# Rows of x loaded first, state-space discretisation merged and moved behind the first norm, first two weight tiles interleaved

## The chip, the cores and the metric

The kernel runs on one core of one Trainium2 chip. The metric is device time in microseconds (us), the median of several runs of the whole program. A core has TensorE (PE, the matmuls), VectorE (DVE), ScalarE (ACT), GpSimd (POOL) and SyncE (SP), each with a program of its own; SP only issues DMAs here.

## The reference

Two transformer-like blocks over 1024 tokens of width 1024, float32 throughout. The part that the change touches is the start of the first block: 16 meta tokens are put ahead (1040 rows), an RMS norm, the input projection, and a state-space branch on its first 512 columns:

```python
h = rmsnorm(x, g_pre)                 # x * rsqrt(mean(x*x) + eps) * g
proj = h @ w_in
u, q, k, v, o, gi, gf, ga, gb = jnp.split(proj, IN_SPLITS, axis=-1)
dt = exp(log_dt); mag = exp(lam_re * dt)          # s5_ssm: "discretisation"
ab_re, ab_im = mag * cos(lam_im * dt), mag * sin(lam_im * dt)
z = ((ab - 1) * conj(lam)) / |lam|^2;  bb = z * b # complex
x_t = ab * x_(t-1) + bb u_t                       # complex scan over the tokens
y_a = gelu(Re(c x_t) + d * u_t);  y_a *= sigmoid(y_a @ w_glu)
```

Behind it come an mLSTM, branch and output projections, a gated feed-forward part with a convolution, and a second block (RWKV, dilated attention, feed-forward). Nothing of those is touched.

## The kernel before

**Tiling.** Activations lie transposed, 128 features on the partitions and 1040 columns of tokens, in `HB[:, k, :]` for k = 0..7. The columns are cut in three chunks c0, c1, c2 of 264, 264 and 512 (`CH1`). A dense product goes by tiles of 128 output features: a 512 KB weight tile `w_raw` comes by DMA from SP, ScalarE rounds it to `w_hi` (`split_act`), VectorE takes the rest `w_lo = w_raw - w_hi` (`split_dve`), and TensorE makes three matmuls for each k (hi·hi, hi·lo, lo·hi), 24 for a chunk and 72 for a tile. There are two `w_raw` and three `w_hi`/`w_lo` buffers. The input projection (`IN1`) has 24 tiles, t0 to t23: four u, four v, four o, eight q/k (t12 to t19), four g; then one tile "gates", then the tiles of the glu.

**The norm.** `prenorm_act` squares each row block of x in three chunks into one of the six-chunk temporaries (`ssm_VX`, `m_S`, `m_S`, `m_G`), `prenorm_pe` sums over the partitions with a matrix of ones, ScalarE takes the root in two steps (Ln, Exp), VectorE makes y = x·g·root into a temporary, ScalarE copies it rounded into `XHA`/`XHB`, and VectorE writes the rest into `XLA`/`XLB`. c0 and c1 lie in XHA/XLA, c2 in XHB/XLB.

**The first tiles.** t0, t1, t2 are run as nine groups in the order of `FIRST`: c0 of all three, c1 of all three, c2 of all three, so that TensorE can start while the norm of c1 and c2 is still made.

**The state-space branch** rides in the background. It is a generator for each engine (`ssm_pe`, `ssm_act`, `ssm_dve`); every chunk of the main work calls `tick()`, which runs RS = 3 steps, up to the next three `yield`s. What lies between two yields is issued as a piece, and each engine executes its instructions in the order issued. `pause(n)` skips n steps, and PRE, MID and POST set how long. On VectorE the generator makes the discretisation ("one" with 16 columns, "two" with 256), `bb`, `Bn`, the table E of powers over 130 blocks (into HB), then for each group j = 0..3 of u: `powers(j)`, `outputs(j)` (the array `ssm_W`), `ssm_Dop`, and the X chain with the scan. ScalarE turns them into the matmul operands `ssm_Bop` (`inputs`) and `ssm_Cop` (`outputs`), copies the results "bu" and applies the gelu. TensorE has three pieces for each j: "k" (16 matmuls of `ssm_Cop` and `ssm_Bn`), "bu" (64) and "ys" (eight steps of 2 to 16 matmuls on `ssm_Dop` and `ssm_Cop`).

**Order and waits at the start.** POOL issues the eight row blocks of x; SP issues `ssm_p1`, `ssm_p2` (640 KB), waits for x3, and then issues the first two weight tiles and `ssm_bc1`; ScalarE issues `cst` (612 KB, with the matrix of ones and the identity) and `vecs`. `step()` calls inside the norm put the discretisation between its squares; on VectorE all of it stands ahead of the two first `w_lo`. The DVE program of `first_dve` ticks nine times, 27 steps, before it takes `w_lo` of t3 and later tiles. A q or k tile goes through one buffer `m_G`: ScalarE evicts the three chunks into it, VectorE convolves (one TENSOR_SCALAR, three SCALAR_TENSOR_TENSOR over 1040 columns), and the next tile's eviction waits for that. PSUM has a ring of four banks for the dense chunks and one of four for the background.

## Time and profile before

| | us |
|---|---|
| median of 3 runs | 3365.61 (3361.63 to 3368.23) |
| the profiled execution | 3363.58 |
| its span | 3361.8 |
| TensorE busy in it | 3217.5 (96%) |
| VectorE busy | 1713.1 (51%) |
| ScalarE busy | 1219.6 (36%) |
| POOL busy | 74.6 (2%) |
| mean granted TensorE clock | 0.99 |

Times inside the trace are counted from the span's start. A timeline row is: start, duration, engine, line, operation, what it writes and reads, the form (partitions x elements), how many in a row, and in brackets how long the engine stood idle before and who released it. The listing with its line numbers is the one printed above. A float32 or fp32r matmul shows as one or more records in the trace.

### The profile page before, as it was taken

The numbers are of one execution on the slowest core, as the hardware profiler recorded it, in microseconds if no ns is written. First come the engines' busy times: TensorE is split into PE (matmuls) and PEld (weight loads), VectorE is DVE, ScalarE is ACT, GpSimd is POOL, SyncE is SP. The second block draws the span as 40 slices with busy tenths as digits, with TensorE's granted clock in tenths as the row PEclk, the third lists the DMA queues.
The fourth block names the chain that finished last, engine by engine and source line by source line (L and its number), as shares of the span: only waits on it lengthen the run. The fifth ranks groups of instructions, "written<-read, shape, count | busy, mean of one in ns | idle before, by whom it ended". The sixth has DMA issues, their size and how long they took to land.

```text
span 3361.8 us, 56145 instructions
## 1 busy us (share of the span) xinstructions
PE 3217.5 (96%) x24028; PEld 2678.6 (80%) x24028; DVE 1713.1 (51%) x3196; ACT 1219.6 (36%) x2166; POOL 74.6 (2%) x148
## 2 busy tenths in 40 slices
...
GB/s 106 60 68 64 67 86 66 77 58 139 160 107 90 55 49 46 51 44 82 136 177 157 125 86 93 29 23 24 18 14 119 94 91 54 46 50 45 55 94 113
DMA packets 85624, 262.36 MB, mean 78 GB/s; under 512 B 10592, under 2 KB 10720, under 8 KB 85248
## 3 DMA queue, kind: packets, MB, share of 16 engines
...
q14 instruction: 58, 0.48, 0.0%
...
## 4 chain that ended last, share of the span: by engine, by line
PE 79%; DVE 11%; ACT 7%; issue 2%; DMA 1%; DVEq 0%; SPq 0%; POOL 0%; ACTq 0%; POOLq 0%
PE ps L127 76%; PE ps L126 2%; DVE HB L166 2%; DVE w_lo L166 1%; PE ps L135 1%; ACT w_hi L163 1%; ACT L145 1%; DVE HB L176 1%; ACT m_D L145 1%; DVE C L176 1%; ACT a_PT L163 0%; DVE m_SS L176 0%; DVE XLA L166 0%; DMA m_D<-mq 0%; ACT L150 0%
## 5 line engine op out<-in xcount | busy, mean ns | idle before, releaser
L166 DVE TENSOR_TENSOR w_lo<-w_raw,w_hi 128x1024 fp32r<-128x1024 f32 (+3 forms) x353 | 393.5, 1115 | 384.2 <-ACT w_hi L163 382.1
L127 PE MATMUL ps<-XHA,w_hi 128*128 128x264 f32 (+3 forms) x1456 | 467.8, 321 | 37.4 <-DVE w_lo L166 33.2
L163 ACT ACTIVATE w_hi<-w_raw 128x1024 fp32r<-128x1024 f32 (+3 forms) x353 | 339.9, 963 | 340.9 <-PE ps L127 281.2
L127 PE MATMUL ps<-XLA,w_hi 128*128 128x264 f32 (+3 forms) x1456 | 457.7, 314 | 0.0
L127 PE MATMUL ps<-XHA,w_lo 128*128 128x264 f32 (+3 forms) x1456 | 456.2, 313 | 0.0
L127 PE MATMUL ps<-XHB,w_hi 128*128 128x512 f32 x920 | 369.9, 402 | 6.4 <-DVE w_lo L166 3.7
L127 PE MATMUL ps<-XHB,w_lo 128*128 128x512 f32 x920 | 360.2, 391 | 0.0
L127 PE MATMUL ps<-XLB,w_hi 128*128 128x512 f32 x920 | 360.1, 391 | 0.0
L127 PEld LDWEIGHTS ps<-XHA,w_hi 128*128 128x128 f32 x1456 | 276.3, 190 | 68.4 <-issue 43.3
L127 PEld LDWEIGHTS ps<-XLA,w_hi 128*128 128x128 f32 x1456 | 276.2, 190 | 21.1 <-issue 3.6
L127 PEld LDWEIGHTS ps<-XHA,w_lo 128*128 128x128 f32 x1456 | 276.6, 190 | 16.5
L127 PEld LDWEIGHTS ps<-XHB,w_hi 128*128 128x128 f32 x920 | 173.6, 189 | 49.7 <-issue 9.4
L127 PEld LDWEIGHTS ps<-XHB,w_lo 128*128 128x128 f32 x920 | 173.5, 189 | 37.2
L127 PEld LDWEIGHTS ps<-XLB,w_hi 128*128 128x128 f32 x920 | 173.7, 189 | 36.0 <-issue 1.9
L166 DVE TENSOR_TENSOR HB<-HB,ps 128x512 f32<-128x512 f32 (+1 forms) x136 | 88.5, 655 | 213.0 <-PE ps L127 213.0
L127 PE MATMUL ps<-X2HA,w_hi 128*128 128x512 f32 x416 | 163.6, 393 | 2.1 <-DVE w_lo L166 2.1
L127 PE MATMUL ps<-X2HB,w_hi 128*128 128x512 f32 x416 | 162.7, 391 | 0.0
L127 PE MATMUL ps<-X2LA,w_hi 128*128 128x512 f32 x416 | 162.5, 391 | 0.0
L127 PE MATMUL ps<-X2HA,w_lo 128*128 128x512 f32 x416 | 162.4, 390 | 0.0
L127 PE MATMUL ps<-X2HB,w_lo 128*128 128x512 f32 x416 | 161.9, 389 | 0.0
L127 PE MATMUL ps<-X2LB,w_hi 128*128 128x512 f32 x416 | 161.8, 389 | 0.0
L173 DVE TENSOR_SCALAR C<-G,vecs 128x512 f32<-128x512 f32 x88 | 48.0, 546 | 212.8 <-ACT G L163 212.8
...
## 6 DMA issues: line engine op xcount, KB each, us to landing
...
```

The costliest lines, as they stand in the source:

```text
L126: return Issued(e.matmul(out, a, b, start=start, stop=stop, skip_group_check=True))
L127: return Issued(e.matmul(out, a, b, start=start, stop=stop))
L135: return Issued(self.eng and self.eng.transpose(out, src, ident))
L145: return Issued(self.eng and self.eng.activation(out, src, func, **kw))
L163: return Issued(self.eng and self.eng.activation(out, src, ACT.Copy))
L166: return Issued(self.eng and self.eng.tensor_tensor(out, a, b, op))
L173: return Issued(self.eng.tensor_scalar(out, a, s1, s2, op0, op1))
L176: return Issued(self.eng and self.eng.scalar_tensor_tensor(out=out, in0=a, scalar=s, in1=b, op0=op0, op1=op1))
```

## The change

**Loads.** SP issues x0, x2, x4, the first weight tile, x6, the second, the merged parameters `ssm_p2` (680 KB), the third tile, and `ssm_bc1`. ScalarE issues x1, x3, x5, x7 and `vecs`. `cst` is loaded by POOL once x6 and x7 have landed. The ones are written by a VectorE memset.

**Norm.** Each row block is squared whole (x7 in three chunks) into buffers of its own, `squares`, which overlay the later X area. VectorE adds the squares of x2 and x3, and of x4 and x5, so that the sums take 18 matmuls in place of 24. The first root comes ahead of the copies, the second and third stand between them, and so do the splits of t1 and t2. One table load stands at the start; the two parts of the discretisation brought four others.

**Discretisation.** "One" and "two" are one array of ND = 272 columns, treated once. It is no longer in the norm: the DVE generator starts behind it, and is cut in short steps (`cmul_steps` yields twice within a complex product).

**Ticks.** `first_dve` ticks only for c2: three ticks, nine steps, before `w_lo` of t3. PRE goes from 42 to 82, POST from 8 to 4, EASE = 2 is new, and the pauses around `inputs(0)` and `outputs(0)` are new.

**First tiles.** `first_order` runs t0 and t1 in c0 interleaved: four k of t0, then t0 and t1 by turns, then four k of t1. The eight matmuls ahead of them are 128 columns wide, on the ones, in place of 256 on the identity.

```diff
-LAG, K0, RS, RM, NG, PRE, MID, POST, HN, Q5 = 9, 1, 3, 5, 4, 42, 18, 8, 8, 1
+LAG, RS, RM, NG, PRE, MID, POST, HN, Q5 = 9, 3, 5, 4, 82, 18, 4, 8, 1
+EASE = 2
...
+def cmul_steps(V, S, outr, outi, ar, ai, br, bi, t1, t2):
+    V.tt(outr, ar, br, MUL).then_inc(S)
+    a = V.tt(t1, ai, bi, MUL).then_inc(S)
+    yield
+    V.tt(outi, ar, bi, MUL).then_inc(S)
+    b = V.tt(t2, ai, br, MUL).then_inc(S)
+    yield
+    V.wait_ge(S, a)
+    V.tt(outr, outr, t1, SUB).then_inc(S)
+    V.wait_ge(S, b)
+    V.tt(outi, outi, t2, ADD).then_inc(S)
...
+SUMS = [(0,), (1,), (2, 3), (4, 5), (6,), (7,)]
...
-    for k in range(8):
+    P.wait_ge(S.dve, "ones")
+    for n, ks in enumerate(SUMS):
+        k = ks[0]
         for c, (c0, cn) in enumerate(CH1):
-            n, b = K.tmp1.take(P, k, False)
-            P.wait_ge(S.act, ("sq", k, c))
-            P.mm(K.fg["pn", "sum", c][:, 0:cn], K.ones, b[:, 0:cn], k == 0, k == 7).then_inc(S.pe, ("sq", k, c))
-        P.step(K0)
+            P.wait_ge(S.act, ("sq", ks[-1], c))
+            if len(ks) > 1:
+                P.wait_ge(S.dve, ("pair", k))
+            op = P.mm(K.fg["pn", "sum", c][:, 0:cn], K.ones, K.squares[k][:, c0:c0 + cn], n == 0, n == len(SUMS) - 1)
+            if n == len(SUMS) - 1:
+                op.then_inc(S.pe, ("sum", c))
...
 def prenorm_act(A, K):
     S = K.pn
-    A.step(3)
+    A.table(LN_EXP)
     for k in range(8):
         A.wait_ge(K.x[k], "x")
-        for c, (c0, cn) in enumerate(CH1):
-            n, b = K.tmp1.take(A, k, True)
-            A.act(b[:, 0:cn], K.HB[:, k, c0:c0 + cn], ACT.Square).then_inc(S.act, ("sq", k, c))
-            K.tmp1.done(n, (S.pe, ("sq", k, c)))
-        A.step(K0 if k < 5 else 0)
-        if k in FIRST_W:
-            split_act(A, K, FIRST_W.index(k))
-    A.table(LN_EXP)
+        for n, (c0, cn) in enumerate(CH1 if k == 7 else [(0, T1)]):
+            A.act(K.squares[k][:, c0:c0 + cn], K.HB[:, k, c0:c0 + cn], ACT.Square).then_inc(S.act, ("sq", k, n))
+        if k < 7:
+            S.act.at["sq", k, 1] = S.act.at["sq", k, 2] = S.act.n
+        if k == 5:
+            split_act(A, K, 0)
+    A.wait_ge(K.c.pool, END)
...
+        A.wait_ge(S.pe, ("sum", c))
...
+    def between(c, k):
+        if c == 0 and k == 1:
+            split_act(A, K, 1)
+        if c == 0 and k in (4, 6):
+            root(k // 2 - 1)
+        if c == 0 and k == 7:
+            split_act(A, K, 2)
+            s = ssm_views(K)
+            A.wait_ge(K.ssm_ld, END)
+            A.act(s.dt, s.p[:, 2, :], ACT.Exp).then_inc(K.ssm.act, "dt")
+
     root(0)
-    root(1)
     for c, (c0, cn) in enumerate(CH1):
-        normalise_act(A, K, S, c, c0, cn, K.tmp1)
-        if c == 0:
-            root(2)
-            split_act(A, K, 2)
+        for k in range(8):
+            n, b = K.tmp1.take(A, k, False)
+            A.wait_ge(S.dve, ("y", c, k))
+            A.cp(S.X.hi(k, c0, cn), b[:, 0:cn]).then_inc(S.act, ("hi", c, k))
+            between(c, k)
...
-    V.step(8 * K0)
-    for i in range(2):
-        split_dve(V, K, i)
-    K.tmp1.n[V] = 24
-    for k in range(8):
-        V.wait_ge(K.x[k], "x")
+    for a, b in ((2, 3), (4, 5)):
+        V.wait_ge(S.act, ("sq", b, 0))
+        V.tt(K.squares[a], K.squares[a], K.squares[b], ADD).then_inc(S.dve, ("pair", a))
+    split_dve(V, K, 0)
...
+        if c == 0 and k == 3:
+            split_dve(V, K, 1)
...
+ND = 272
...
 def ssm_sp(D, K):
-    D.dma(K.ssm_p1[:, :, :], K.I["ssm_p1"]).then_inc(K.ssm_ld, by=16)
-    D.dma(ssm_views(K).p2, K.I["ssm_p2"]).then_inc(K.ssm_ld, by=16)
-    D.wait_ge(K.x[3], "x")
+    for k in (0, 2, 4):
+        D.dma(K.HB[:, k, 0:T1], K.I["x1"][:, k, :]).then_inc(K.x[k], "x", by=16)
     load_weight(D, K, 0)
+    D.dma(K.HB[:, 6, 0:T1], K.I["x1"][:, 6, :]).then_inc(K.x[6], "x", by=16)
     load_weight(D, K, 1)
+    D.dma(K.ssm_BT[:, 0:3 * ND + 512], K.I["ssm_p2"]).then_inc(K.ssm_ld, by=16)
+    load_weight(D, K, 2)
     D.dma(K.ssm_bc1[:, :, :, :], K.I["ssm_bc1"]).then_inc(K.ssm_bl, by=16)
...
+def discretise_act(A, K, S, s):
+    A.wait_ge(S.dve, "den")
+    A.act(s.mag, s.den, ACT.Exp).then_inc(S.act, "mag")
+    yield from pause(22)
+    for name, out in (("sn", s.sn), ("cs", s.cs)):
+        A.wait_ge(S.dve, name)
+        A.act(out, out, ACT.Sin).then_inc(S.act, name)
     yield
-    A.wait_ge(S.dve, (tag, "den"))
-    A.act(mag, den, ACT.Exp).then_inc(S.act, (tag, "mag"))
-    for name, out in (("sn", sn), ("cs", cs)):
-        A.wait_ge(S.dve, (tag, name))
-        A.act(out, out, ACT.Sin).then_inc(S.act, (tag, name))
-        yield
...
+def discretise_dve(V, K, S, s):
...
+    V.tt(zr, lr, lr, MUL).then_inc(d)
+    V.tt(kc, li, li, MUL).then_inc(d)
...
+    V.recip(den, den).then_inc(d)
+    yield
+    V.wait_ge(S.act, "cs")
...
-    yield
-    yield from pause(10)
-    while P.hold:
-        yield
-    yield from pause(8)
     yield from pause(PRE)
...
+    yield from discretise_act(A, K, S, s)
...
-    yield from pause(8)
-    yield from pause(33)
+    yield from pause(PRE - 23 - 11)
     inputs(0)
-    yield from pause(8)
+    yield from pause(9)
     outputs(0)
-    yield from pause(PRE - 41)
+    yield from pause(2)
...
+    yield from discretise_dve(V, K, S, s)
+    one = lambda a: a[:, 256:ND]
+    two = lambda a: a[:, 0:256]
+    mag1, c1, n1, ar1, ai1, zr1, zi1 = [one(a) for a in (s.mag, s.cs, s.sn, s.ar, s.ai, s.zr, s.zi)]
+    ar2, ai2, zr2, zi2 = [two(a) for a in (s.ar, s.ai, s.zr, s.zi)]
+    V.after(d)
+    yield from cmul_steps(V, d, K.ssm_bb2[:, 0, :], K.ssm_bb2[:, 1, :], zr2, zi2, s.b2[:, 0, :], s.b2[:, 1, :], q1[:, 0, :], q1[:, 1, :])
     yield
-    yield from discretise_dve(V, K, S, "one", K.ssm_p1[:, 0, :], K.ssm_p1[:, 1, :], s.one)
...
-    cmul(V, d, K.ssm_bb2[:, 0, :], K.ssm_bb2[:, 1, :], zr2, zi2, s.p2[:, 3, :], s.p2[:, 4, :], q1[:, 0, :], q1[:, 1, :])
...
+    V.wait_ge(K.c.cst, END)
+    yield from cmul_steps(V, d, sq(K.ssm_bb1[:, 0, :]), sq(K.ssm_bb1[:, 1, :]), b16(zr1), b16(zi1), bc1[:, 0], bc1[:, 1],
+                          sq(q1[:, 0, :]), sq(q1[:, 1, :]))
+    yield
...
-    yield
-    while V.hold:
-        yield
...
-    def outputs(j):
+    def outputs(j, often):
...
-            if tau % 2 == 1:
+            if often or tau % 2 == 1:
                 yield
     yield from powers(0)
-    yield from pause(23)
-    yield from outputs(0)
-    yield from pause(PRE - 38)
+    yield from outputs(0, True)
+    yield from pause(EASE)
...
+def first_order():
+
+    both = [(0, 0, k) for k in range(4)]
+    for k in range(4, 8):
+        both += [(0, 0, k), (0, 1, k - 4)]
+    both += [(0, 1, k) for k in range(4, 8)]
+    return both + [(c, t, k) for c, t in FIRST[2:] for k in range(8)]
...
-    for n, (c, t) in enumerate(FIRST):
+    begun = []
+    for c, t, k in first_order():
...
+        if (c, t) not in begun:
+            b = first_ring(K, len(begun)).take(P, ("u", t, c))
+            if not begun:
+                for _ in range(8):
+                    P.mm(b[:, 0:128], K.ones, K.ones, True, True)
+            begun.append((c, t))
+            P.wait_ge(K.w.act, ("hi", i))
+            P.wait_ge(K.w.dve, ("lo", i))
+        b = first_ring(K, FIRST.index((c, t)))["u", t, c]
+        ready(k, c)
+        x, y = K.X.hi(k, c0, cn), K.X.lo(k, c0, cn)
+        P.mm(b[:, 0:cn], wh[:, k, :], x, k == 0, False)
+        P.mm(b[:, 0:cn], wh[:, k, :], y, False, False)
+        op = P.mm(b[:, 0:cn], wl[:, k, :], x, False, k == 7)
+        if k == 7:
+            op.then_inc(S.pe, ("u", t, c))
+            K.used[i] = (S.pe, ("u", t, c))
+            P.tick()
+            P.u_done += c == 2
+    P.wait_ge(K.c.cst, END)
...
 def first_dve(V, K):
     next_tile(V, K, split_dve)
     for c, t in FIRST:
-        V.tick()
+        if c == 2:
+            V.tick()
...
-    for i in (2, 3, 4):
+    for i in (3, 4):
...
-    for k in range(8):
-        G.dma(K.HB[:, k, 0:T1], K.I["x1"][:, k, :]).then_inc(K.x[k], "x", by=16)
     G.mset(K.small[:, 0:1], 1e-6).then_inc(K.c.pool)
     G.mset(K.small[:, 1:2], 64e-5).then_inc(K.c.pool)
     G.mset(K.small[:, 2:3], 1.0).then_inc(K.c.pool)
     G.mset(K.small[:, 4:6], 0.0).then_inc(K.c.pool)
     G.mset(K.G1[:, 0:3], 0.0).then_inc(K.gpad)
+    G.wait_ge(K.x[6], "x")
+    G.wait_ge(K.x[7], "x")
+    G.dma(K.cst[:, 256:1224], K.I["cst"][:, 256:1224]).then_inc(K.c.cst, by=16)
+    G.dma(K.cst[:, 0:128], K.I["cst"][:, 0:128]).then_inc(K.c.cst, by=16)
     G.wait_ge(K.c.cst, END)
...
 def act_program(A, K):
-    A.dma(K.cst[:, :], K.I["cst"]).then_inc(K.c.cst, by=16)
+    for k in (1, 3, 5, 7):
+        A.dma(K.HB[:, k, 0:T1], K.I["x1"][:, k, :]).then_inc(K.x[k], "x", by=16)
     A.dma(K.vecs[:, :], K.I["vecs"]).then_inc(K.c.vec, by=16)
+    prenorm_act(A, K)
+    A.wait_ge(K.c.vec, END)
     A.bg.append(ssm_act(A, K))
-    A.step()
-    A.wait_ge(K.c.pool, END)
-    A.wait_ge(K.c.vec, END)
-    prenorm_act(A, K)
-    A.hold, A.rate = False, RS
+    A.rate = RS
...
 def dve_program(V, K):
+    V.mset(K.ones, 1.0).then_inc(K.pn.dve, "ones")
+    prenorm_dve(V, K)
     V.bg.append(ssm_dve(V, K))
-    V.step()
-    V.wait_ge(K.c.cst, END)
-    V.wait_ge(K.c.vec, END)
-    prenorm_dve(V, K)
-    V.hold, V.rate = False, RS
+    V.rate = RS
...
-    o["ssm_p1"] = np.stack([one(lr), one(li), one(ldt)], axis=1)
...
-    o["ssm_p2"] = np.stack([rep(lr), rep(li), rep(ldt), o2(bre), o2(bim)], axis=1)
+    o["ssm_p2"] = np.concatenate([f(a) for a in (lr, li, ldt) for f in (rep, one)] + [o2(bre), o2(bim)], axis=1)
```

**VectorE, the first `w_lo` behind the norm.** `ssm_W` is what `powers(0)` writes. Before, the end of `powers(0)` and four `w_lo` in a row:

```order
L166 TENSOR_TENSOR ssm_W<-ssm_W,ssm_q 128x64 [waits s_ssm_dve] x2
L166 TENSOR_TENSOR ssm_W<-ssm_W,ssm_a 128x64 [waits s_ssm_dve]
L166 TENSOR_TENSOR ssm_q<-ssm_W,ssm_a 128x64
L166 TENSOR_TENSOR ssm_W<-ssm_W,ssm_a 128x64
L166 TENSOR_TENSOR ssm_q<-ssm_W,ssm_a 128x64
L166 TENSOR_TENSOR ssm_W<-ssm_W,ssm_q 128x64 [waits s_ssm_dve] x2
L166 TENSOR_TENSOR w_lo<-w_raw,w_hi 128x1024 [waits s_w_act] x4
L186 COPY ssm_W<-ssm_bc 128x64 [waits s_ssm_dve,s_ssm_act]
```

In the changed kernel, the discretisation of 272 columns and the first `w_lo` behind the norm:

```order
L167 TENSOR_TENSOR ssm_Cop<-ssm_BT 128x272 x2
L167 TENSOR_TENSOR ssm_Cop<-ssm_Cop 128x272 [waits s_ssm_dve,s_ssm_act]
L184 RECIPROCAL ssm_Cop<-ssm_Cop 128x272 [waits s_ssm_dve]
L167 TENSOR_TENSOR w_lo<-w_raw,w_hi 128x1024 [waits s_w_act]
L167 TENSOR_TENSOR ssm_a<-ssm_Cop 128x272 [waits s_ssm_act]
L167 TENSOR_TENSOR ssm_a<-ssm_Cop 128x272
L173 TENSOR_SCALAR ssm_Cop<-ssm_a 128x272 [waits s_ssm_dve]
L167 TENSOR_TENSOR ssm_Cop<-ssm_Cop,ssm_BT 128x272 [waits s_ssm_dve]
```

`w_lo` of t3 stood behind the whole of E and `powers(0)`, 162 rows behind the norm's last; now it stands 18 rows behind it, and one `w_lo` comes every few rows.

**ScalarE, the squares.** `ssm_VX`, `m_S` and `m_G` are the temporaries of the squares, `ssm_Cop` is the discretisation's scratch. Before:

```order
L145 ACTIVATE ssm_VX<-HB 128x264 [waits s_x_in0]
L145 ACTIVATE ssm_VX<-HB 128x264
L145 ACTIVATE m_S<-HB 128x512
L145 ACTIVATE m_S<-HB 128x264 [waits s_x_in1]
L145 ACTIVATE m_G<-HB 128x264
L145 ACTIVATE m_G<-HB 128x512
L145 ACT_TABLE_LOAD
L145 ACTIVATE ssm_Cop<-ssm_BT 128x256
L145 ACTIVATE ssm_VX<-HB 128x264 [waits s_pn_pe,s_x_in2]
L145 ACTIVATE ssm_VX<-HB 128x264 [waits s_pn_pe]
L145 ACTIVATE m_S<-HB 128x512 [waits s_pn_pe]
L145 ACTIVATE ssm_Cop<-ssm_Cop 128x256 [waits s_ssm_dve]
```

Changed:

```order
L151 ACT_TABLE_LOAD
L146 ACTIVATE squares<-HB 128x1040 [waits s_x_in0]
L146 ACTIVATE squares<-HB 128x1040 [waits s_x_in1]
L146 ACTIVATE squares<-HB 128x1040 [waits s_x_in2]
L146 ACTIVATE squares<-HB 128x1040 [waits s_x_in3]
L146 ACTIVATE squares<-HB 128x1040 [waits s_x_in4]
L146 ACTIVATE squares<-HB 128x1040 [waits s_x_in5]
L164 ACTIVATE w_hi<-w_raw 128x1024 [waits s_w_raw0]
L146 ACTIVATE squares<-HB 128x1040 [waits s_x_in6]
L146 ACTIVATE squares<-HB 128x264 [waits s_x_in7]
L146 ACTIVATE squares<-HB 128x264
L146 ACTIVATE squares<-HB 128x512
```

The discretisation's activations and table loads are gone from between the squares, and a row block is one instruction.

**TensorE, the piece k of j = 0.** With row numbers, since the matmuls read alike. Before, behind the last chunk of t5 and ahead of the first of t6:

```order
453 L127 MATMUL ps<-XLB,w_hi 128x512
454 L127 MATMUL ps<-XHB,w_lo 128x512
455 L126 MATMUL ps<-ssm_Cop,ssm_Bn 32x256 [waits s_ssm_dve,s_ssm_act]
456 L126 MATMUL ps<-ssm_Cop,ssm_Bn 32x256 x7
457 L127 MATMUL ps<-XHA,w_hi 128x264 [waits s_w_dve,s_w_act,s_in1_act]
458 L127 MATMUL ps<-XLA,w_hi 128x264
```

Changed, inside t9, behind its c0:

```order
689 L128 MATMUL ps<-XLA,w_hi 128x264
690 L128 MATMUL ps<-XHA,w_lo 128x264
691 L127 MATMUL ps<-ssm_Cop,ssm_Bn 32x256 [waits s_ssm_dve,s_ssm_act]
692 L127 MATMUL ps<-ssm_Cop,ssm_Bn 32x256 x7
693 L128 MATMUL ps<-XHA,w_hi 128x264 [waits s_in1_act]
694 L128 MATMUL ps<-XLA,w_hi 128x264
```

The piece moved from between two tiles to behind the first chunk of a tile, more than three tiles later.

## Rows read from the trace of the kernel before

**Rows 1.** TensorE waits, 34 to 650 us: us in total, times, longest us.
```profile
PE ps L127 <- DVE w_lo L166: 27.7, 1, 27.7
...
PE ps L126 <- ACT ssm_Cop L145: 3.7, 1, 3.7
PE ps L127 <- DVE ssm_Dop L186: 2.8, 2, 1.5
```

**Rows 2.** Windows: busy us of each engine, TensorE clock, DMA share, GB/s.
```profile
18.00:20.00 2.00, 2.00 (x8) 1.32 (x7) 1.79 (x7) 1.62 (x3) 0.00 (x0) 1.00 1.03 412
20.00:22.00 2.00, 2.00 (x9) 1.21 (x8) 1.83 (x6) 1.56 (x4) 0.00 (x0) 1.00 0.13 49
...
80.00:90.00 10.00, 0.00 (x0) 0.00 (x0) 9.80 (x36) 0.00 (x0) 0.00 (x0) 0.50 0.00 0
99.00:103.00 4.00, 3.81 (x17) 3.84 (x18) 1.18 (x2) 0.56 (x1) 0.00 (x0) 0.50 0.69 203
...
138.00:144.00 6.00, 4.84 (x29) 3.57 (x30) 3.17 (x6) 2.06 (x2) 0.00 (x0) 0.50 0.40 144
212.00:276.00 64.00, 64.00 (x625) 56.13 (x624) 41.22 (x128) 19.23 (x30) 0.00 (x0) 1.00 0.19 67
```

**Rows 3.** Timeline of TensorE at the start: start us, us, line, operation.
```profile
15.21 2.79 PE L127 MATMUL ps<-m_S,cst 128*128 128x512 f32 x4
...
20.29 1.47 PE L127 MATMUL ps<-m_S,cst 128*128 128x512 f32 x4
...
34.22 0.36 PE L127 MATMUL ps<-XHA,w_hi 128*128 128x264 f32 x1
```

**Rows 4.** Timeline of ScalarE at the start.
```profile
9.86 1.28 ACT L145 ACT_TABLE_LOAD   x1
11.18 0.21 ACT L145 ACTIVATE ssm_s<-ssm_s 128x16 f32<-128x16 f32 x1
...
28.79 0.93 ACT L145 ACTIVATE m_G<-HB 128x264 f32<-128x264 f32 x2
...
31.04 0.48 ACT L145 ACTIVATE m_S<-ps,small 128x264 f32<-128x264 f32 x1
```

**Rows 5.** DMA issues up to 40 us: KB each, us to landing.
```profile
HB<-in_x POOLq DMA_DIRECT2D x8, 520.0 KB, 9.4
```

**Rows 6.** Timeline of VectorE at the start.
```profile
16.91 0.43 DVE L166 TENSOR_TENSOR ssm_Cop<-ssm_BT,ssm_Cop 128x256 f32<-128x256 f32 x1 [1.69 <-ACT ssm_Cop L145]
...
22.50 0.29 DVE L173 TENSOR_SCALAR ssm_Cop<-ssm_Cop 128x256 f32<-128x256 f32 x1
...
25.27 1.75 DVE L183 RECIPROCAL ssm_Cop<-ssm_Cop 128x256 f32<-128x256 f32 x1
...
32.66 0.89 DVE L176 SCALAR_TENSOR_TENSOR ssm_VX<-HB,vecs,m_S 128x264 f32<-128x264 f32 x2
```

**Rows 7.** Timeline of VectorE, 57 to 100 us.
```profile
57.48 1.47 DVE L166 TENSOR_TENSOR XLB<-m_G,XHB 128x512 fp32r<-128x512 f32 x2
...
97.83 2.35 DVE L166 TENSOR_TENSOR w_lo<-w_raw,w_hi 128x1024 fp32r<-128x1024 f32 x2
```

**Rows 8.** Timeline of ScalarE around 136 us.
```profile
135.48 0.60 ACT L145 ACTIVATE m_S<-ps 128x512 f32<-128x512 f32 x1 [5.09 <-PE ps L127]
136.71 1.25 ACT L145 ACTIVATE ssm_Cop<-ssm_W,cst 128x1152 f32<-128x1152 f32 x1 [0.63 <-DVE ssm_W L166]
```

**Rows 9.** Timeline of VectorE, 299 to 350 us.
```profile
306.39 1.31 DVE L166 TENSOR_TENSOR ssm_BT<-ssm_BT,HB 128x520 f32<-128x520 f32 x2 [1.04 <-ACT ssm_BT L163]
...
317.27 0.07 DVE L192 MEMSET ssm_VX<- 128x8 f32 x1
...
332.17 0.20 DVE L186 COPY ssm_W<-ssm_bc 128x64 f32<-128x64 f32 x1 [2.25 <-ACT ssm_Bop L145]
...
341.73 3.98 DVE L176 SCALAR_TENSOR_TENSOR m_S<-m_G,vecs,m_S 128x1040 f32<-128x1040 f32 x3
```

**Rows 10.** Timeline of ScalarE, 322 to 358 us.
```profile
354.36 2.40 ACT L145 ACTIVATE ssm_Cop<-ssm_W,cst 128x1152 f32<-128x1152 f32 x2
```

More of the change, by code:

```diff
@@ L512, in prenorm_dve @@
     for c, (c0, cn) in enumerate(CH1):
         V.wait_ge(S.act, ("sd", c))
-        normalise_dve(V, K, S, K.HB, K.rs0, c, c0, cn, "g_mix_pre", K.tmp1)
+        for k in range(8):
+            n, b = held[k] = tmp.take(V, k, True)
+            V.stt(b[:, 0:cn], K.HB[:, k, c0:c0 + cn], K.vec("g_mix_pre", k), K.rs0[:, c0:c0 + cn], MUL, MUL).then_inc(
+                S.dve, ("y", c, k))
+            if k:
+                rest(c, k - 1, c0, cn)
+        rest(c, 7, c0, cn)
         if c == 0:
@@ L668, in ssm_act @@
     S, s = K.ssm, ssm_views(K)
-    yield
-    yield from discretise_act(A, K, S, "one", K.ssm_p1[:, 2, :], s.one)
-    yield from discretise_act(A, K, S, "two", s.p2[:, 2, :], s.two)
-    yield from pause(2)
-    while A.hold:
-        yield
+    yield from discretise_act(A, K, S, s)
     def inputs(j):
@@ L778, in ssm_dve @@
             V.after(d)
-            cmul(V, d, E[:, 0, at, n:n + k], E[:, 1, at, n:n + k], E[:, 0, at, 0:k], E[:, 1, at, 0:k], bc(cur[0]), bc(cur[1]),
-                 qa, qb)
+            many = cmul_steps if w * k > 200 else cmul_whole
+            yield from many(V, d, E[:, 0, at, n:n + k], E[:, 1, at, n:n + k], E[:, 0, at, 0:k], E[:, 1, at, 0:k],
+                            bc(cur[0]), bc(cur[1]), qa, qb)
         n += k
@@ L883, in ssm_dve @@
             yield from pause(3)
-            yield from outputs(j + 1)
+            yield from outputs(j + 1, False)
             yield from pause(MID - 18)
```

91 lines of the change are left out of this document (39 added, 52 removed), and 2 rows, old and new, of the table WARM.

## The prediction

> **What bounds the kernel now.** I read the busy shares first: TensorE is busy for 96% of the span and every other engine for about half or less, so TensorE sets the end, and the change can only gain what TensorE waits for or runs slowly through. All that is changed lies ahead of the glu, which TensorE begins at about 444 us; from there on the order of all engines is the same. So I read TensorE's waits from its first real matmul on [rows 1]: one of 27.7 us for a `w_lo`, one of 3.7 for `ssm_Cop`, two of 2.8 together for `ssm_Dop`. Then the start: the first real matmul is at 34.22 [rows 3], which is time without product work. Then the clock: TensorE is granted 0.50 in the windows at 80, 99 and 138 us [rows 2], thus 1.2 in place of 2.4 GHz, each time around a wait of rows 1. The sum is made against the profiled execution, 3363.6 us, which is 2.0 below the median of the three runs shown and inside their spread.
>
> **A: the start.** The rows of x come at 412 GB/s with the DMA share at 1.03, and by 20 to 22 us the share is down to 0.13 [rows 2]. But the last square begins at 28.79 [rows 4]: before, ScalarE is what is late, since the discretisation's activations and table loads stand between the squares and wait for VectorE. Now nothing stands there, so the end of the loads decides. Ahead of x6 on the queues are eight rows of x at 520 KB [rows 5], one weight tile and `vecs`, 4.9 MB; at 0.41 MB per us, from 2.7 us on (an estimate: at that pace the 7.2 MB of rows, parameters, constants and first two tiles are over at 20 us, as they are), and with 0.7 us to land, x6 is there at 15.3. Behind it: its square over 1040 columns, 1.1 (0.93 for the 776 columns of [rows 4], scaled); its sums, 1.9 (1.47 for 776 columns at full clock [rows 3]); the first chunk of x7's sums, 0.4; the root, 0.9, and hand-overs, 0.1; from the first y at 32.66 [rows 6] to the first matmul at 34.22 [rows 3], 1.6. That gives 21.3 in place of 34.22: **-12.9**. Bounds: 19.5, if x6 lands ahead of its share; 25, if the sums run at half clock to their end, as the first ones did (2.79 in place of 1.47 [rows 3]), and the row loads come no better than with everything else between them (20.2 us for all).
>
> On the two queues: the traffic ran at 412 GB/s with all row loads on one of them. The Trainium skill, "DMA: Bandwidth & Descriptors", section "Issuing engines are not separate DMA queues", says that issuing from several engines saves only the time of the issue; by that rule the split between SP and ScalarE gives nothing, and I book nothing for it. What term A books is the order: 2.2 MB of parameters, constants and later tiles leave the front.
>
> **B: the nine groups of t0 to t2.** They end at 71.5 (the wait of 27.7 begins there, as the `w_lo` pair at 97.83 takes 2.35 [rows 7]), 37.3 behind the first matmul. VectorE gets one more `w_lo` (2.35/2) into the norm of c0, and ScalarE gets two roots and a split between its copies. Interleaving t0 and t1 puts TensorE's work where the norm of c0 sets the pace, and gives some back. I take **+1.3**; bounds 0 and +2.4.
>
> **C: the wait of 27.7.** VectorE's norm ends at 58.9 [rows 7], and then 39 us of `bb`, E and powers stand ahead of `w_lo` of t3. Now it is 18 rows. Their price: the 256-column steps of "two" went from 16.91 to 22.79, 5.9 for 16 instructions [rows 6]; scaled by 272/256 6.1; three products and a sum more, 1.1; the RECIPROCAL 1.75 [rows 6]: 9.0. With the first matmul as zero the norm ends at 24.7 + 1.2 (the added `w_lo`) + 1.2 (waits for ScalarE) = 27.1, `w_lo` starts at 36.1 and ends at 37.3, and the nine groups end at 38.6. So it is there 1.3 ahead of need, and the next ones have a tile's time each (11.3) for under ten rows of work. The whole wait goes: **-27.7**; bound: 3 of it stay, if ScalarE's Exp or its `w_hi` comes late. **D:** behind the wait TensorE ran at 0.50 from 99.2 to 103 [rows 2]; without the idle time there is no drop: half of 3.8 us, **-2.0**.
>
> The 39 us of VectorE are not gone. They now run beside t3 to t8, and `outputs(0)` behind them. Six tiles are 68 us of TensorE, and before, VectorE was busy for 1.18 of the 4 us behind 99 [rows 2] and had `outputs(0)` and one split a tile up to 137. That is the cover.
>
> **E: k and Dop of j = 0.** Cop(0) is issued behind the c2 eviction of a tile (135.48) and was 0.63 late by VectorE at 136.71, then takes 2.4 [rows 8]; k stood at the tile's end and waited 3.7. Now k has one chunk of 264 columns, 2.9 us, between: 0.8 stays, **-2.9**. The window of 138 to 144 at 0.50 has 4.84 us of TensorE work [rows 2]: half of it, **-2.4**. The two waits for Dop, at the first ys, go, as ys is now over two tiles behind k: **-2.8** [rows 1].
>
> **F: what is late next.** PRE moves k, bu, ys by some three to four tiles, so that j = 1 and 2 fall into the q/k tiles t13 to t20, where VectorE also convolves and where the next tile's eviction waits for it. VectorE in such a stretch is busy for 41.2 of 64 us [rows 2]; enough in sum, but its order is fixed. I followed the order of the three engines with: X chain 11.0 (306.39 to 317.37), outputs 8.7 (332.17 to 340.9), convolution 4.9 (0.9 and the 3.98 of 341.73), Cop 2.4 [rows 9, 10], a table load of 1.3 from its start to the next activation's [rows 4]. With t9's start as zero, X(1) is done at 98, t14's convolution at 107.5, outputs(2) at 121.4, t15's convolution at 126.3, t16's at 134.2; then eviction, table load, gelu, and Cop(2) is done at 139.0. TensorE comes to k(2) at 135.4: it waits **+3.6**, and I take the clock drop of E again behind it, **+2.4**. k(1) and two bank waits behind convolutions: **+1.7**. Bounds for all of F: 0 and 14.
>
> The table load is 1.28, and the next activation begins 1.32 behind its start [rows 4]. The Trainium skill, "ScalarE: Activation LUTs", section "What ACT_TABLE_LOAD costs", adds a drain and gives 2.66 for each switch. By that page k(2) would wait 1.4 longer, and the sum would be 3323.3; here the trace disagrees with it.
>
> **Sum.** -12.9 + 1.3 - 27.7 - 2.0 - 2.9 - 2.4 - 2.8 + 3.6 + 2.4 + 1.7 = -41.7, and 3363.6 - 41.7 = **3322**.
>
> **Rivals.**
> 1. *F does not arise.* A few us of slack in VectorE's chain (a convolution that starts when its tile's eviction is done) let Cop(2) come in time. For: my count has hand-overs that overlap in the trace. Then 3322 - 7.7 = 3314.
> 2. *The start gains less.* The loads of weights and parameters share the bandwidth with the rows, and the sums run at half clock, since TensorE has less to do there (18 matmuls, not 24). For: the first sums at half clock [rows 3]. First matmul at 27 to 29 in place of 21.3: 3328 to 3330.
> 3. *The wait is not gone but moved.* `w_lo` of t3, or one of the next, still comes late by 5 to 15 us, as a short step behind it waits for ScalarE's Exp or Sin, which wait in ScalarE's own order behind an eviction. For: VectorE waits for ScalarE more than once ahead of t4's `w_lo`. Against: each takes 0.4 and a table load 1.3. 3330 to 3340.
> 4. *Slower than before.* The moved work is serialised with TensorE in the q/k stage. A q/k tile's convolution stands behind the X chain (11.0) and outputs (8.7 and the wait for Bop), the next tile's eviction behind the convolution, and TensorE has four banks, 13 us of chunks, ahead. If VectorE falls behind by over 13 us of slack, TensorE pays both blocks, about 20 us, in each of three j: 60, and the time is 3322 + 60 = 3382. Against: VectorE's four convolutions, X chain, powers, outputs and splits of one j are 52.5 us of 61.5. It decides once waits add 9 us to each j.
> 5. *Nothing moves* (the 27.7 are given back in a lump at the drain behind t23, where ys(3) now stands): the ys work is the same in either place, so this would need the last gelu to be late. 3355 to 3370.
>
> **How the numbers follow.** Forecast 0.50; rival 1 0.18; rival 2 0.16; rival 3 0.10; rival 4 0.03; rival 5 0.03. From 3308 (rival 1 and x6 early) to 3338 (rival 3 but for its end) holds all but about 0.12; the size of F and A is worked out from single rows, so I do not make it narrower. A difference under 0.2%, 6.7 us, is about what a measurement of this kernel cannot tell from none. Faster by more: all but rivals 4 and 5, and part of the latter, 0.95; within: 0.02; slower: 0.03.
>
> **What the profile of the changed kernel would show.** The first real matmul at 21 us, the last row's square ending by about 17 (A). No wait of TensorE for a `w_lo` above 1 us and clock 1.00 from the third tile on (C, D). `w_lo` of t3 at about 57 (B, C). The wait for `ssm_Cop` in two or three places with 0.5 to 4 us, the largest at the third k, and a window at 0.50 behind it (E, F). From the glu on, every tile at the same distance as before. The forecast is wrong if a wait for m_G or m_S evictions of several us turns up on TensorE between t12 and t20, or if the first matmul is behind 25 us.

## The result

| | before | changed |
|---|---|---|
| median, us (4 runs each) | 3363.62 (3360.52 to 3368.23) | 3321.56 (3317.30 to 3322.42) |
| ratio | | 0.9875 (95%: 0.986 to 0.989) |
| the profiled execution | 3363.58 | 3317.30 |
| its span | 3361.8 | 3315.2 |
| first real matmul | 34.22 | 21.38 |
| t0 to t2 done, t3 begins | 71.5, and 99.19 behind the wait | 59.38 |
| first matmul of the glu | 443.86 | 403.2 |

By the medians 42 us are gone, where 41.7 were forecast. By the first matmul of the glu, behind which no order of work changed, it is 40.7. The page's first part of the changed kernel, busy us, share of the span and instructions:

```profile
PE 3205.0 (97%) x24016; PEld 2668.3 (80%) x24016; DVE 1711.8 (52%) x3168; ACT 1207.9 (36%) x2140; POOL 71.5 (2%) x142
```

TensorE's share goes from 96 to 97%. Its waits from its first sums to 650 us (us in total, times, longest), which answer to [rows 1]:

```profile
PE ps L127 <- ACT ssm_Cop L146: 5.2, 3, 4.1
...
PE ps L128 <- DVE glu_l L167: 1.9, 2, 1.5
...
PE ps L128 <- ACT m_G L146: 1.5, 2, 0.8
PE ps L127 <- DVE ssm_VX L193: 1.4, 1, 1.4
PE ps L128 <- ACT XHA L164: 1.3, 1, 1.3
```

(`...` stands for lines left out.) No wait for a `w_lo` is left in this stretch, and none for `ssm_Dop`. `ssm_Cop` is now waited for three times, 4.1 us at the most. Windows (busy us of each engine, TensorE clock, DMA share, GB/s), which answer to [rows 2]:

```profile
14.00:16.00 2.00, 2.00 (x8) 1.14 (x6) 1.23 (x1) 1.31 (x3) 0.77 (x2) 1.00 1.04 414
25.00:28.00 3.00, 2.45 (x11) 2.48 (x12) 2.05 (x7) 2.55 (x6) 0.00 (x0) 0.52 0.49 175
60.00:100.00 40.00, 40.00 (x265) 36.93 (x264) 35.13 (x145) 10.59 (x16) 0.00 (x0) 1.00 0.25 93
100.00:130.00 30.00, 30.00 (x189) 27.20 (x188) 20.85 (x115) 9.96 (x14) 0.00 (x0) 1.00 0.21 77
270.00:275.00 5.00, 5.00 (x27) 3.65 (x27) 2.03 (x5) 0.05 (x1) 0.00 (x0) 0.66 0.00 0
```

TensorE is busy from 60 to 130 us without a gap at full clock. There VectorE is busy for 35.13 of 40 us: the 39 us of table and powers that TensorE waited for. Two windows are at half clock for a part: in c0 at 25 us and behind the third k at 270 us.

The start, on TensorE, ScalarE and VectorE (start, us, engine, line, operation), which answers to [rows 3], [rows 4] and [rows 6, 7]:

```profile
6.58 13.26 PE L128 MATMUL ps<-squares,cst 128*128 128x264 f32 x36 [6.58 <-ACT squares L146]
19.68 1.95 PE L128 MATMUL ps<-cst 128*128 128x128 f32 x16
21.38 0.37 PE L128 MATMUL ps<-XHA,w_hi 128*128 128x264 f32 x1
```

```profile
14.95 2.22 ACT L146 ACTIVATE squares<-HB 128x1040 f32<-128x1040 f32 x4 [0.69 <-DMA HB<-in_x]
18.64 0.48 ACT L146 ACTIVATE m_S<-ps,small 128x264 f32<-128x264 f32 x1 [1.47 <-PE ps L128]
```

```profile
46.78 0.44 DVE L167 TENSOR_TENSOR ssm_Cop<-ssm_BT,ssm_Cop 128x272 f32<-128x272 f32 x1
...
54.12 1.85 DVE L184 RECIPROCAL ssm_Cop<-ssm_Cop 128x272 f32<-128x272 f32 x1
55.89 1.16 DVE L167 TENSOR_TENSOR w_lo<-w_raw,w_hi 128x1024 fp32r<-128x1024 f32 x1
```

The last squares, of x6 and x7, begin at 14.95, and the root waits 1.47 us, for TensorE's sums, which run from 6.58 to 19.84 without a gap. The part of the discretisation that stands ahead of `w_lo` of t3 takes 46.78 to 55.89, 9.1 us (its last products come behind it), and `w_lo` of t3 is written 2.3 us before t3 can begin.

### The profile page after: what moved, and what is told of

Read it like the earlier page. It is cut to its first block, busy times and chain, and to the rows that moved or that the text cites. A ratio compares the mean times of both kernels' runs of the same rounds, so it can differ in the third digit from the quotient of the medians.

```text
span 3315.2 us, 56059 instructions
## 1 busy us (share of the span) xinstructions
PE 3205.0 (97%) x24016; PEld 2668.3 (80%) x24016; DVE 1711.8 (52%) x3168; ACT 1207.9 (36%) x2140; POOL 71.5 (2%) x142
## 4 chain that ended last, share of the span: by engine, by line
PE 79%; DVE 11%; ACT 7%; issue 2%; DMA 1%; DVEq 0%; SPq 0%; POOL 0%; ACTq 0%; POOLq 0%
PE ps L128 76%; PE ps L127 2%; DVE w_lo L167 1%; DVE HB L167 1%; PE ps L136 1%; ACT w_hi L164 1%; ACT L146 1%; DVE HB L177 1%; ACT m_D L146 1%; DVE m_S L177 1%; DVE C L177 1%; ACT a_PT L164 0%; DVE m_SS L177 0%; DMA m_D<-mq 0%; DVE ssm_q L167 0%
```

## The experiments

The times of before beside which each run was made had medians of 3359.6 to 3361.9. Since executions of one kernel spread over 2 to 11 us, I compare, beside the medians, three marks of each trace, where an edit at the start shows undisturbed: the first real matmul, the start of t3, and the first matmul of the glu (changed kernel: 21.38, 59.38, 403.2). There is one trace of each run, and the marks scatter too: four of the runs below (short steps undone, and the three on the places of k) leave the start as it is in the changed kernel, and together with it they have the first real matmul at 21.38 to 21.88 and t3 at 59.38 to 60.07. A difference of up to 0.7 us in these marks shows nothing.

### The ticks alone

```diff
 def first_dve(V, K):                    # the kernel before
     for c, t in FIRST:
-        V.tick()
+        if c == 2:
+            V.tick()
 def ssm_pe(P, K):
-    yield from pause(PRE)
+    yield from pause(PRE + 18)
 def ssm_act(A, K):
-    yield from pause(33)
+    yield from pause(33 + 18)
```

> The kernel before with one part of the change: VectorE's background ticks in the first nine groups only for c2 (9 steps ahead of w_lo of t3, not 27), and the TensorE and ScalarE pieces of the state-space work put 18 steps later to match. Loads, norm, discretisation, interleaving as before. My theory (terms C and D): the wait of 27.7 us for w_lo and its clock drop go, since 9 steps of bb, Bn and the first powers are about 10 us and VectorE is free at 58.9 against a need at 71.5; the 3.7 us wait for Cop(0) stays, as all is shifted alike; but the steps of E are long ones (9 steps of 1.7 to 2.8 us in a tile of 11.3), so up to 5 us come back at t4 to t6. About 3363.6 - 29.7 + 2 = 3336 (3333 to 3340). Rival (the merge and the short steps are what matters): waits of 10 us or more in t4 to t8, 3345 or above.

Measured: 3334.62 us (3333.47 to 3335.98), ratio 0.9917 (0.9902 to 0.9932). TensorE's waits up to 460 us:

```profile
PE ps L126 <- ACT ssm_Cop L145: 3.7, 1, 3.7
PE ps L126 <- DVE ssm_VX L192: 1.9, 1, 1.9
...
PE ps L127 <- DVE ssm_Dop L186: 1.5, 1, 1.5
```

No wait for `w_lo` at all, not even with long steps: `w_lo` of t3 starts at 68.20 and takes 1.22, and t3 begins at 71.32. The first real matmul stays at 34.22, and the glu begins at 415.5, 381.3 behind it; before it was 409.6, in the changed kernel 381.8. So 28 us of the gain (27.2 by the medians) come from one `if`, the number of steps ahead of `w_lo` of t3, with two pauses to match, and the merge, the short steps and the other places of k add nothing there. The tick edit without the two pauses was not tried; as I read the order, TensorE would then wait for Cop(0) with tiles held that VectorE's steps need to get on.

### Short steps undone

```diff
 def cmul_steps(V, S, outr, outi, ar, ai, br, bi, t1, t2):    # the changed kernel
-    V.tt(outr, ar, br, MUL).then_inc(S)
-    ...
+    cmul(V, S, outr, outi, ar, ai, br, bi, t1, t2)
+    yield
+    yield
```

> The changed kernel with whole complex products in one step again (the two yields of cmul_steps behind the product, so that the count of steps is the same). If nine steps and not their length are what brought w_lo of t3 in time, nothing moves: no wait of TensorE for w_lo, glu within 0.5 us of 403.2. Rival (the short steps are needed to get each w_lo out in time): waits for w_lo of 1 to 3 us at t4 to t8.

Measured: 3321.73 us (3316.10 to 3324.85), glu at 403.4, the same waits as the changed kernel's to 0.1 us. As expected, nothing moved. A whole product of 256 columns is some 2.1 us, and no wait for a `w_lo` came of it.

### The loads in the old order, and all on one queue

```diff
 def ssm_sp(D, K):                       # e3: the changed kernel
+    D.dma(K.ssm_BT[:, 0:3 * ND + 512], K.I["ssm_p2"]).then_inc(K.ssm_ld, by=16)
+    D.wait_ge(K.x[3], "x")
-    for k in (0, 2, 4):
-        D.dma(K.HB[:, k, 0:T1], K.I["x1"][:, k, :]).then_inc(K.x[k], "x", by=16)
...
 def act_program(A, K):
-    for k in (1, 3, 5, 7):
-        A.dma(K.HB[:, k, 0:T1], K.I["x1"][:, k, :]).then_inc(K.x[k], "x", by=16)
+    A.dma(K.cst[:, 256:1224], K.I["cst"][:, 256:1224]).then_inc(K.c.cst, by=16)
...
 def pool_program(G, K):
+    for k in range(8):
+        G.dma(K.HB[:, k, 0:T1], K.I["x1"][:, k, :]).then_inc(K.x[k], "x", by=16)
```

> The changed kernel with the loads in the old order: all rows of x on POOL, constants on ScalarE and the state-space parameters on SP at the very start. If the order of the bytes is what term A gained at the loads, the last row lands at about 19 to 20 us, the first real matmul is at 25 to 26 in place of 21.4, and the time is 4 to 5 us above the changed kernel's. Rival (ScalarE, not the loads, set the start in both kernels, so A came from taking the discretisation out of the squares): first matmul within 1 us of 21.4 and the same time.

```diff
 def ssm_sp(D, K):                       # e4: the changed kernel
-    for k in (0, 2, 4):
+    for k in range(6):
...
-    D.dma(K.HB[:, 6, 0:T1], K.I["x1"][:, 6, :]).then_inc(K.x[6], "x", by=16)
+    for k in (6, 7):
+        D.dma(K.HB[:, k, 0:T1], K.I["x1"][:, k, :]).then_inc(K.x[k], "x", by=16)
```

> The changed kernel with all eight rows issued by SP, in the same order of bytes (x0 to x5, first weight tile, x6, x7), none by ScalarE. If the queue does not matter, the DMA share stays near 1.0 at 410 to 430 GB/s, the first matmul is within 0.5 us of 21.4 and the time is the same. Rival (two queues share the bandwidth better or issue earlier): the first matmul 1 us or more later.

The first real matmul of the one and of the other:

```profile
25.79 0.37 PE L128 MATMUL ps<-XHA,w_hi 128*128 128x264 f32 x1
```

```profile
20.97 0.37 PE L128 MATMUL ps<-XHA,w_hi 128*128 128x264 f32 x1
```

Old order: 3326.06 us (3323.46 to 3328.85), first matmul 4.4 later, glu at 407.3, 4.1 later. One queue: 3322.19 us (3318.80 to 3322.84), first matmul 0.4 sooner. So of the 12.8 us of term A the order of the loads is 4.4; the other 8.4 stay with the old loads, and belong together to what no longer stands between the squares and to the fewer sums; no run takes these two apart. Both expectations held. The second queue is worth nothing. The Trainium skill, "DMA: Bandwidth & Descriptors", section "Issuing engines are not separate DMA queues", says that several issuing engines save no more than the time of the issue, and the trace agrees (20.97 with one, 21.38 with two).

### The sums of the squares

```diff
-SUMS = [(0,), (1,), (2, 3), (4, 5), (6,), (7,)]        # e12: the changed kernel
+SUMS = [(k,) for k in range(8)]
```

> The changed kernel without VectorE's additions of squares: 24 sum matmuls in place of 18. By term A the end of the start is set by what lands last (x6, x7), and 6 more sums of 0.6 us each ahead of them are done as the rows land: the first real matmul within 0.7 us of 21.4. Rival (TensorE is behind with its sums at half or full clock): 1 to 3 us later.

```diff
 def prenorm_pe(P, K):                   # e11: the changed kernel
-    for n, ks in enumerate(SUMS):
-        for c, (c0, cn) in enumerate(CH1):
+    last = len(SUMS) - 1
+    walk = ([(n, c) for n in range(last - 1) for c in range(3)]
+            + [(n, c) for c in range(3) for n in (last - 1, last)])
+    for n, c in walk:
```

> The changed kernel with the last sums by chunk: x6 and x7 for c0, then for c1, then for c2, in place of all of x6 and then all of x7. Term A has the whole of x6's sums (1.8 us) between its square and the first root. If TensorE's sums are what the first root waits for (1.47 us in the changed kernel), it comes up to 1.3 us sooner, as x7's first square is there by then: first real matmul at 20.2 to 20.8. Rival (x7's square is what is late): first matmul within 0.3 us of 21.4.

TensorE's start in the run without pairs, and in the run by chunk, and ScalarE's first root in each:

```profile
6.87 16.90 PE L128 MATMUL ps<-squares,cst 128*128 128x264 f32 x48 [6.87 <-ACT squares L146]
...
25.31 0.37 PE L128 MATMUL ps<-XHA,w_hi 128*128 128x264 f32 x1
```

```profile
22.57 0.48 ACT L146 ACTIVATE m_S<-ps,small 128x264 f32<-128x264 f32 x1 [5.12 <-PE ps L128]
```

```profile
20.12 1.95 PE L128 MATMUL ps<-cst 128*128 128x128 f32 x16
21.82 0.37 PE L128 MATMUL ps<-XHA,w_hi 128*128 128x264 f32 x1
```

```profile
17.77 0.48 ACT L146 ACTIVATE m_S<-ps,small 128x264 f32<-128x264 f32 x1 [0.17 <-PE ps L128]
```

Without pairs: 3326.93 us (3326.43 to 3330.73), the first root waits 5.12 us for the sums, and the first real matmul is 3.9 us later (0.3 of it in a later first square), the glu, at 407.2, 4.0. My expectation was wrong, and the rival's cause came about, beyond the 1 to 3 us that it gave: 24 sums keep TensorE busy for 16.9 us without a gap from its first square on, and end 6.3 us behind the last square. So two VectorE additions of 1.24 us are worth some 3.6 to 3.9 us, which I had booked at nothing. It is TensorE's own pace that counts here, and its first sums are slow in every trace. In the changed kernel:

```profile
7.00:11.00 4.00, 4.00 (x8) 2.41 (x8) 0.85 (x1) 2.78 (x4) 0.00 (x0) 1.00 1.02 419
13.00:17.00 4.00, 4.00 (x15) 2.53 (x14) 2.18 (x2) 3.10 (x5) 1.24 (x2) 1.00 1.04 419
```

Busy all the time in both windows, it gets 8 records done in the first and 15 in the second, while the granted clock reads 1.00 in both. The prediction calls such sums "at half clock"; the rows show half the pace, and not its cause.

By chunk: 3319.22 us (3315.42 to 3323.86), the root waits 0.17 in place of 1.47, and yet the first real matmul is at 21.82, where I had expected 20.2 to 20.8. The first `XLA` piece is ready at 20.25, but the matmul stands behind the warm-up matmuls, which stand behind all sums: TensorE's own queue is what is late. In the changed kernel these two are nearly level (the piece is ready at 21.10, the matmul starts at 21.38). VectorE's norm still began sooner, so that t3 begins at 58.35 and the glu at 402.6.

### The interleaving, and the clock in c0

```diff
 def first_order():                      # e5: the changed kernel
-    both = [(0, 0, k) for k in range(4)]
-    ...
+    both = [(0, t, k) for t in range(2) for k in range(8)]
```

> The changed kernel with t0 and t1 one after the other in c0 (the order of before), all else as changed. If interleaving gives TensorE work while the norm of c0 sets its pace, the nine groups end 1 to 2.9 us later than 59.4 and the time is as much longer, unless the clock drop at 25 us changes. Rival (the norm of c1 and c2 on VectorE sets the end of the nine groups anyway): nothing moves by more than 0.5 us.

Measured: 3323.04 us (3318.71 to 3325.20). The glu is at 405.8, 2.6 us later, and t3 begins 40.7 us behind the first matmul, in place of 37.8 to 38.2. But the trace shows half clock from 26.7 to 33.6 us, and from 28.6 on TensorE waits for nothing until t3, so that up to 2.5 us of the difference can be the clock. So the interleaving is worth 0.4 to 2.9 us by this trace, and whether the longer drop comes of the order itself no run shows; the medians can't tell either.

```diff
 def first_pe(P, K, ready):              # e8: the changed kernel
+        if (c, t, k) == (0, 0, 4):
+            early = first_ring(K, 1).take(P, ("u", 1, 0))
+            for _ in range(12):
+                P.mm(early[:, 0:128], K.ones, K.ones, True, True)
```

> The changed kernel with twelve matmuls of 128 columns on the ones (1.5 us, their result is overwritten) between the fourth and fifth k of t0, where TensorE idles for 1.29 us, the last of several gaps in c0, and falls to half clock from 25.1 to 28.5. If the gap brings the drop, the window at 25 to 28 shows 1.00 and the nine groups end up to 1.7 us sooner. Rival (VectorE's and ScalarE's norm sets the pace there at either clock): clock 1.00 but the nine groups end within 0.5 us of 59.4.

```profile
25.00:28.00 3.00, 3.00 (x29) 3.00 (x28) 2.21 (x6) 2.24 (x5) 0.00 (x0) 1.00 0.52 175
```

```profile
24.42 2.84 PE L128 MATMUL ps<-cst 128*128 128x128 f32 x24
```

3318.44 us (3316.71 to 3322.43). The clock stays at 1.00, and the twelve took 2.84 us, nearly twice what I had priced; t3 begins at 59.53 and the glu at 403.3, the same. That the gap brings the drop does not follow, though. The two runs below with the pieces later, and with k alone later, have the start of the changed kernel to the letter, with the same gap and no drop. The same place in the first of them:

```profile
25.77 0.36 PE L128 MATMUL ps<-XHA,w_hi 128*128 128x264 f32 x1 [1.28 <-ACT XHA L164]
```

```profile
25.00:28.00 3.00, 2.23 (x18) 2.26 (x18) 2.12 (x6) 2.33 (x6) 0.00 (x0) 1.00 0.55 175
```

Of the five traces with this start three show a drop there and two none. And it costs little: t3 begins 38.0 to 38.2 us behind the first matmul with the drop, 37.8 without it, and 37.8 in this run, with neither drop nor gap. So the rival held: up to here the norm sets the pace, at either clock.

### The places of k, bu and ys

```diff
 def ssm_pe(P, K):                       # e6 (e7: PRE - 3), the changed kernel
-    yield from pause(PRE)
+    yield from pause(PRE + 3)
```

> The changed kernel with TensorE's state-space pieces one chunk later (pause(PRE + 3) in ssm_pe alone). The third k waits 4.1 us for Cop(2) in the changed kernel, and TensorE runs 3.4 us at half clock behind it (term F). With the chunk of c2 (5.5 us) between, the waits for Cop of 5.2 us in all should be 0 to 0.5 and the drop behind the third k gone: the glu begins 4 to 7 us sooner than at 403.2, time about 3316. Rival (the wait moves: ScalarE's copies of bu and the evictions behind them, or the X chain, are then what is late): the same sum of waits under other names, glu within 1 us of 403.2.

> The changed kernel with TensorE's state-space pieces one chunk sooner (pause(PRE - 3) in ssm_pe alone), so that k(0) stands at the end of a tile as in the kernel before. By term E, k(0) then waits 3.7 us as before, with a clock drop of 3.4 to 6.8 us behind it that costs 1.7 to 3.4; k(1) and k(2) each come one chunk sooner and wait 3 to 6 us longer. Glu 8 to 15 us later than at 403.2, time 3330 to 3337. Rival (the wait for Cop is absorbed, since the wait of the first shifts all that follows): glu 3 to 4 us later.

TensorE's waits in the run with the pieces later, then with them sooner:

```profile
PE ps L128 <- ACT m_G L146: 8.6, 2, 6.2
```

```profile
PE ps L127 <- ACT ssm_Cop L146: 24.5, 4, 7.8
```

Later: 3326.19 us (3321.66 to 3327.58), glu at 405.4. Sooner: 3348.09 us (3345.12 to 3353.31), glu at 430.8. Both are worse than the changed kernel, and both expectations were wrong in size, the first (glu 4 to 7 us sooner) in its sign too. Later, all waits for `ssm_Cop` are gone, but 8.6 us for evictions of `m_G` come in. The chain of work before the longer of them (start, us, what; left out are VectorE's steps of the X chain and powers):

```profile
288.68 1.22 ACT ssm_BT L164 x4
...
303.94 0.74 DVE m_S L174
...
308.72 0.40 ACT m_G L146
```

bu of j = 2 ends at 288.7, then the copies, X chain and powers to 303.9, the convolution, and the eviction for which the bank is held. Sooner, all four k wait, 3.7, 5.5, 7.8 and 7.5 us, 24.5 in place of 5.2; I had put the glu 8 to 15 us later, and it is 27.6. That the fourth would wait at all I had not seen.

```diff
 def ssm_pe(P, K):                       # e10: the changed kernel
+        yield from pause(3)
         b = K.sb.take(P, ("k", j))
...
-        yield from pause(3)
         first = K.sb.take(P, ("bu", j, 0))
 def ssm_dve(V, K):
-        yield from pause(3)
+        yield from pause(6)
         V.wait_ge(S.pe, ("k", j))
...
-        yield from pause(4)
-        yield from pause(2)
+        yield from pause(3)
```

> The changed kernel with TensorE's piece k alone one chunk later, right ahead of bu, which stays in its place with ys; VectorE's copies of k into ssm_Dop stand three steps later to match. The run with all pieces later showed that bu must not come later (X chain, convolution, eviction follow it) while k waits for Cop. If that is right, the waits for Cop (5.2 us) and the drop behind the third k (1.7) go and the waits for m_G evictions stay at 1.5: glu 5 to 7 us sooner than at 403.2, time about 3315. Rival (VectorE's Dop work put later delays its convolution or the X chain): waits for m_G of 3 us or more, glu within 2 us of 403.2.

```profile
PE ps L128 <- DVE ssm_Dop L187: 8.2, 3, 4.4
...
PE ps L128 <- ACT m_G L146: 1.5, 2, 0.8
```

3324.04 us (3322.16 to 3325.47), glu at 407.5. I had expected 3315. The theory was half right: no wait for `ssm_Cop`, none more for `m_G`. But bu takes the bank that k used, so it waits for VectorE's copies of k, 8.2 us. The chain at the third k is Cop, k, copies, bu, and the chunk between k and bu is not spare.

### A version for the start

```diff
                                         # e13: e11 and e8 together, and
 def first_pe(P, K, ready):
-            if not begun:
-                for _ in range(8):
-                    P.mm(b[:, 0:128], K.ones, K.ones, True, True)
```

> A version meant to beat the changed kernel at the start: the last sums by chunk, no warm-up matmuls ahead of the first real one (they held it back from 20.3 to 21.8 in the run with the sums by chunk, while the first XLA piece was ready at 20.3), and the twelve dummy matmuls in the gap of c0. If TensorE's own queue set the first real matmul, it comes at 20.2 to 20.6, the clock stays at 1.00 up to the third k, and the nine groups end 0.8 to 1.5 us sooner than at 59.4, the glu at 402 to 402.5. Rival (the norm's pace sets the end of the nine groups, and the clock falls without the warm-up): nine groups at 59 to 60, a window at 0.50 between 18 and 28. In time this is 0.03%, below what the runs can tell; the verdict is in the trace.

```profile
20.27 0.36 PE L128 MATMUL ps<-XHA,w_hi 128*128 128x264 f32 x1
```

3321.51 us (3320.66 to 3323.17). The first real matmul is 1.1 us sooner than in the changed kernel, t3 begins at 58.21, 1.2 sooner, and the glu at 401.9, 1.3 sooner; the clock stays full up to the third k without the warm-up. By the trace it is the best start of all the runs; by the median no different from the changed kernel. Nearly all of it is the order of the sums, which alone has t3 at 58.35: without the warm-up the first matmul comes 1.5 us sooner than in that run, and t3 only 0.1, since the norm sets the pace between.

## Why the prediction was right

The forecast of 3322 and its direction held, and so did the mechanism. By the terms, between the two profiled executions:

- **A, the start: forecast -12.9, measured -12.8.** The sum was right to 0.1 us, partly by luck. x6 and x7 were squared from 14.95 on, as worked out, but the cause was mis-named. I took the landing of the last rows for what the start waits for. In the changed kernel's trace TensorE has no gap in its sums at all, and where other traces have one, it stands ahead of the sums of x4 and x5 and not of x6; without the pairs the start comes 3.6 to 3.9 us later with the same loads. So it is TensorE's sums that bound it, at about the time that the landing would give, and the additions, costed at nothing, keep them there. The sums at "half clock" of the bound of 25 and of rival 2 are slow ones at a granted clock of 1.00.
- **B: forecast +1.3, measured +0.75** (38.0 behind the first matmul, 37.25 before), with the clock drop of c0 in it, which I had not foreseen there, and which is 0.1 to 0.4 of it by the traces without one.
- **C: forecast -27.7, measured -27.7.** The step of 9.0 us for the discretisation was 9.1. VectorE came free sooner than I had it, at 25.4 and not 27.1 behind the first matmul, so the slack was 2.3 and not 1.3 us. The ticks-alone run shows that this slack did not even need the new discretisation.
- **D, E and F: forecast -2.4 in all, measured -0.85** from the start of t3 to the glu (344.67 before, 343.82 after). Inside: k(0) waits 0.8, as forecast. The third k waits 4.1, forecast 3.6. k(1) and the two `m_G` waits are 1.8, forecast 1.7. The clock drop behind the third k is there, in this trace and in the eight others in which the third k waits about 4.1, and costs less than forecast here, some 1.7. Not in the forecast: 1.4 us for `ssm_VX` at the last ys, where TensorE has no more tiles of the input projection to run beside it.

The chain of work at the third k, start, us, what, is the one that term F followed:

```profile
264.06 1.31 DVE m_S L177
...
265.40 0.39 ACT m_G L146
...
265.81 1.28 ACT L146
...
267.10 0.39 ACT HB L146
267.49 2.29 ACT ssm_Cop L146 x2
...
269.92 1.07 PE ps L127 x16
```

Convolution, eviction, table load of 1.28, gelu, Cop, k: in this order, with 0.01 us between the table load and the gelu. The Trainium skill, "ScalarE: Activation LUTs", section "What ACT_TABLE_LOAD costs", adds a drain of 1.4 us to each switch of table; by this trace it is not there, as in [rows 4].

**The rivals.** Rival 1 (F does not arise) is refuted by the wait of 4.1. Rival 2 (a later first matmul) did not come about: even with the old loads put back it is at 25.8, and with all 24 sums at 25.3, not at 27 to 29. Rivals 3 and 5 left no trace: no `w_lo` wait, and 1.4 us at the drain. Rival 4, the slower side, did not come about, but the run with the pieces one chunk later shows its mechanism at a small scale: 8.6 us of waits for `m_G` evictions that stand behind a convolution. One chunk cost 2.2 us at the glu on that side and 27.6 on the other, where it is Cop that is late. The changed kernel lies on a narrow ridge between Cop and the convolutions.

**What the profiled pair overstates.** From the glu to the end no engine's order changed, and the waits are the same (for `w_lo` 11.3 us in both, beside the 27.7), yet that stretch took 2917.9 us before and 2912.0 after. Two windows in which the profiled execution of before had fallen to half clock, and the same places of the changed kernel, 41 us earlier:

```profile
950.00:954.00 4.00, 4.00 (x22) 4.00 (x23) 1.92 (x2) 1.40 (x3) 0.00 (x0) 0.57 0.16 35
1028.00:1032.00 4.00, 4.00 (x12) 3.07 (x12) 2.29 (x5) 1.57 (x2) 0.00 (x0) 0.59 0.40 131
```

```profile
909.00:913.00 4.00, 4.00 (x28) 3.44 (x28) 2.30 (x4) 2.01 (x5) 0.00 (x0) 1.00 0.30 112
988.00:991.00 3.00, 3.00 (x15) 2.44 (x14) 1.82 (x2) 1.11 (x2) 0.00 (x0) 1.00 0.00 0
```

These two drops, and two more at 2534 and 2657 us, are in one execution and not in the other. In all, the trace of before has eight drops behind the glu's first matmul and the other four, each of some 1.7 us; that accounts for the 5.9 us between 2917.9 and 2912.0. So the spans differ by 46.6 us, the glu's first matmul by 40.7 and the medians by 42.1. Against the later medians of before (3359.6 to 3361.9) it would be 38 to 40. The change is worth some 38 to 42 us, and that the forecast of 41.7 agrees with the medians to half a us is partly luck.
